# The experts' products of a two-block model in native fp32, on four column strips of TensorE, from raw weights

## What is computed

```python
def swiglu(h, wg, wu, wd):
    return jnp.einsum('...f,fd->...d', jax.nn.silu(h @ wg) * (h @ wu), wd)

def moe_swiglu(h, router, wg, wu, wd):
    ht = h.reshape(B * S, D)                                   # 256 x 1024
    logits = jnp.einsum('td,de->te', ht, router).astype(jnp.float32)
    top_vals, top_idx = lax.top_k(logits, TOP_K)               # TOP_K = 2
    gates = jax.nn.softmax(top_vals, axis=-1)
    ...
    for e in range(N_EXPERTS):                                 # 8
        out = out + dense_gate[:, e:e + 1] * swiglu(ht, wg[e], wu[e], wd[e])
```

## Time and profile before

| | |
|---|---|
| Time, median of 3 runs | 1453.48 us (1453.28 to 1454.73) |
| Span of the profiled execution, first to last instruction | 1449.2 us |
| PE busy / weight loads / DVE / ACT | 1416.9 / 1220.5 / 1104.2 / 905.8 us |
| Granted TensorE clock | 9 or more tenths in each of 40 slices |
| DMA in all | 409.63 MB, mean 283 GB/s |

### The profile page before, as it was taken

One profiled execution on the slowest core, in us unless ns is written; L12 is line 12 of the kernel. 1 busy time (PEld: TensorE's weight loads), 2 busy tenths in 40 slices (PEclk: granted clock), 3 DMA queues, 4 the chain that ended last, 5 costly groups with the idle time before them and its releaser, 6 DMA issues.

```text
span 1449.2 us, 19938 instructions
## 1 busy us (share of the span) xinstructions
PE 1416.9 (98%) x7952; PEld 1220.5 (84%) x7952; DVE 1104.2 (76%) x994; ACT 905.8 (63%) x775; POOL 90.6 (6%) x130
## 2 busy tenths in 40 slices
PE   7999999999998999999999999999999999999998
PEld 6879999897787888888888888888878869788896
DVE  6976454379788889888888888888878894657665
ACT  5664434256647676777777777767766765655653
POOL 3400000034011000000000000000002110000000
PEclk9999999999999999999999999999999999999999
DMA  9569975354569999999999999999999965243341
GB/s 323 165 228 299 330 260 189 118 180 140 210 239 364 382 387 372 357 409 350 379 390 348 401 373 353 406 338 388 387 349 385 390 225 192 88 146 117 117 175 58
DMA packets 120978, 409.63 MB, mean 283 GB/s; under 512 B 7026, under 2 KB 32866, under 8 KB 120912
## 3 DMA queue, kind: packets, MB, share of 16 engines
q1 hardware_dynamic: 114432, 392.32, 73.8%
q0 software_dynamic: 5408, 12.58, 2.7%
q10 hardware_dynamic: 1072, 3.80, 0.7%
HBM read 399.53 MB, written 18.87 MB: 289 GB/s over the span
## 4 chain that ended last, share of the span: by engine, by line
PE 85%; DVE 9%; ACT 3%; DMA 2%; issue 1%; SPq 0%; ACTq 0%; DVEq 0%; POOLq 0%
PE ps L496 22%; PE ps L498 22%; PE ps L497 22%; DVE yT L2047 3%; DVE low L480 2%; PE ps L1190 2%; PE ps L1192 2%; PE ps L1191 2%; PE ps L2749 1%; DMA raw<-in_moe_wu 1%; PE ps L2393 1%; PE ps L1399 1%; PE ps L1397 1%; PE ps L1398 1%; DVE low L486 1%
## 5 line engine op out<-in xcount | busy, mean ns | idle before, releaser
L486 DVE TENSOR_TENSOR low<-raw,high 128x2816 fp32r<-128x2816 f32 (+1 forms) x168 | 516.3, 3089 | 97.1 <-ACT high L475 97.0
L475 ACT ACTIVATE high<-raw 128x2816 fp32r<-128x2816 f32 (+1 forms) x168 | 429.0, 2562 | 108.8 <-PE ps L498 50.5
L496 PE MATMUL ps<-high,xT_hi 128*128 128x512 f32 (+1 forms) x1136 | 419.8, 370 | 8.4 <-DVE low L480 4.2
L498 PE MATMUL ps<-high,xT_lo 128*128 128x512 f32 (+1 forms) x1136 | 415.6, 366 | 0.0
L497 PE MATMUL ps<-low,xT_hi 128*128 128x512 f32 (+1 forms) x1136 | 413.9, 364 | 0.0
L480 DVE TENSOR_TENSOR low<-raw,high 128x2816 fp32r<-128x2816 f32 (+2 forms) x72 | 202.3, 2818 | 74.3 <-ACT high L469 73.1
L496 PEld LDWEIGHTS ps<-high,xT_hi 128*128 128x128 f32 x1136 | 213.3, 188 | 40.6 <-DVE low L480 5.7
L469 ACT ACTIVATE high<-raw 128x2816 fp32r<-128x2816 f32 (+3 forms) x71 | 166.8, 2351 | 117.6 <-PE ps L498 92.0
L497 PEld LDWEIGHTS ps<-low,xT_hi 128*128 128x128 f32 x1136 | 213.6, 188 | 28.0
L498 PEld LDWEIGHTS ps<-high,xT_lo 128*128 128x128 f32 x1136 | 213.1, 188 | 28.3
L496 PE MATMUL ps<-high,eT_hi 128*128 128x512 f32 x352 | 140.7, 400 | 0.0
(11 more groups left out here) (436 smaller groups left out, 1854.0 us busy)
## 6 DMA issues: line engine op xcount, KB each, us to landing
raw<-in_moe_wg SPq DMA_DIRECT2D x64, 1408.0 KB, 8.0
raw<-in_moe_wu SPq DMA_DIRECT2D x64, 1408.0 KB, 9.7
raw<-in_moe_wd SPq DMA_DIRECT2D x48, 1536.0 KB, 8.6
rawb<-in_w_in SPq DMA_DIRECT2D x25, 1024.0 KB, 5.1
raw<-in_w_in SPq DMA_DIRECT2D x16, 1024.0 KB, 9.1
raw<-in_moe_wd SPq DMA_DIRECT2D x16, 1024.0 KB
raw<-in_ffn_wg SPq DMA_DIRECT2D x8, 1408.0 KB, 10.2
raw<-in_ffn_wu SPq DMA_DIRECT2D x8, 1408.0 KB, 9.6
```

The source lines that it names most:

```text
L475: nc.scalar.activation(high[:, j % SPLITS, 0:n], raw[:, j % RAWS, 0:n], ACT.Copy).then_inc(hi_made, 1)
L486: nc.vector.tensor_tensor(low[:, j % SPLITS, 0:n], raw[:, j % RAWS, 0:n], f(high[:, j % SPLITS, 0:n]), ALU.subtract).then_inc(lo_made, 1)
L496: nc.tensor.matmul(out, xh, wh, start=first, stop=False)
L498: return nc.tensor.matmul(out, xl, wh, start=False, stop=last)
```

## The change

The experts' weights are no longer split. Tokens and weights go to TensorE as fp32, an item holds up to 96 tokens, and its stationary operand is a group of 32 tokens. The same 32 tokens are loaded into all four column strips, and each strip moves another quarter of the chunk's columns past them (`by_strips`), so that a PSUM bank holds four column ranges of 32 tokens. The hidden columns are cut 4 x 384 and 4 x 320 (`WIDE`), the down columns 4 x 256. 18 transposes of 128 x 128 turn the hidden values, in two batches (after `j` 8 and `j` 16), and the 8 token transposes follow the second one. The chunks lie in `ering`, eight slots over the former three rings; SP issues chunk `j` when PE has used chunk `j - 8`. Gather products add high and low parts in PSUM. `xs` and `ys` have 13 items of 96 rows.

Beside that: DVE does the whole routing before item 0; the second block's first three chunks are split ahead of `finish` and `add_last_item`; the last item's rows are turned back by 24 fp32 matmuls of 32 rows, and PE waits for `moe_added` 4 ahead of `meta_high`. The eviction's write to `ys` is three DMAs.

```diff
+CAP = 96
+STRIP = 32
+STRIPS, TOKS = P // STRIP, CAP // STRIP
+EXTRA = (2 * T) // (CAP + 1)
...
+WIDE = (384, 320)
+PIECE0 = STRIPS * WIDE[0]
+REST = WIDE[1] - 2 * P
+ESLOTS = 8
+DOWN_N = D // STRIPS
...
+    ering = place("ering", [P, ESLOTS, SLOT], F32, [ring_at])
+    over_spare = [ring_at + ESLOTS * SLOT * 4]
+    y_first = place("y_first", [P, NB, D], F32, over_spare)
+    y_second = place("y_second", [P, NB, D], F32, over_spare)
+    xe = place("xe", [P, KT, CAP], F32, over_spare)
+    drop = place("drop", [P, TOKS, NB, P], F32, over_spare)
...
-    def make_low_item(dve, i, j):
-        dve.wait_ge(hi_made, chunk(i, j + 1))
-        n = words(chunk(0, j))
-        nc.vector.tensor_tensor(low[:, j % SPLITS, 0:n], raw[:, j % RAWS, 0:n], f(high[:, j % SPLITS, 0:n]),
                                 ALU.subtract).then_inc(lo_made, 1)
...
-    def load_item(sp, i, j, src):
-        sp.wait_ge(lo_made, chunk(i, j - RAWS + 1))
-        rows, width = src.shape[1], src.shape[2]
-        sp.dma_start(slot_view(raw, j % RAWS, rows, width), src).then_inc(w_landed[j % RAWS], 16)
...
+            def load_item(i, e, last=False):
+                for j in range(FFN_CHUNKS):
+                    if j == 18 and not last:
+                        load_tokens(i)
+                    sp.wait_ge(w_used, chunk(i, j - ESLOTS + 1))
+                    load_expert(sp, e, j)
...
-            high_upto(MOE0 + 1)
...
+        high2(2)
         finish(n_items, last=True)
-        high2(2)
...
+        pe.wait_ge(moe_added, 4)
...
+            def hidden(i, piece):
+                dve.wait_ge(w_used, chunk(i, 8 * piece + 7) + 1)
+                for t in range(TOKS):
+                    dve.wait_ge(esilu_made, 7 * i + 3 * piece + t + 1)
+                    part = eh[piece][:, t, 0:WIDE[piece]]
+                    nc.vector.tensor_tensor(part, part, ps[:, 3 + t, 0:WIDE[piece]], ALU.mult).then_inc(emult_made, 1)
...
-            low_upto(MOE0 + 5)
-            low_upto(MOE0 + 6)
...
+            def turn_hidden(i, piece):
+                pe.wait_ge(emult_made, MULTS * i + (7 if piece else 3))
+                for jb in range(3):
+                    for t in range(TOKS):
+                        mm = nc.tensor.transpose(ps[:, 3 + jb, t * P:t * P + P], eh[piece][:, t, jb * P:jb * P + P], ident)
+                    mm.then_inc(tp_filled, 1)
...
+            def by_strips(out_of, tokens, weights, n, begins, ends):
+                for s in range(STRIPS):
+                    rows = slice(STRIP * s, STRIP * s + STRIP)
+                    mm = nc.tensor.matmul(out_of(rows), tokens, weights[:, n * s:n * s + n], start=begins, stop=ends, skip_group_check=True)
+                return mm
...
+            def gate_or_up(j):
+                piece, up = j // 8, j // 4 % 2
+                n = WIDE[piece]
+                w = slot_view(ering, j % ESLOTS, 2, STRIPS * n)
+                for k in range(2):
+                    kt = 2 * (j % 4) + k
+                    for t in range(TOKS):
+                        mm = by_strips(lambda rows: ps[rows, 3 * up + t, 0:n], xe[:, kt, STRIP * t:STRIP * t + STRIP], w[:, k, :], n,
+                                       kt == 0, kt == KT - 1)
+                return mm
...
+            def down(j, t, n, tile):
+                w = slot_view(ering, j % ESLOTS, len(DOWN_TILES[j - 16]), D)
+                first = t % 2 * DOWN_N
+                return by_strips(lambda rows: ps[rows, 6 + t // 2, first:first + DOWN_N], eT[:, tile, STRIP * t:STRIP * t + STRIP],
+                                 w[:, n, :], DOWN_N, tile == 0 and t != 1, tile == FT - 1)
...
+                    pe.wait_ge(e_landed[j % ESLOTS], landed(i, j))
+                    gate_or_up(j).then_inc(w_used, 1)
+                    if j == 8:
```

More of the change, by code:

```diff
@@ L431, in model_program, with landed, load_expert, rows @@
     wu_v = a["moe_wu"].rearrange("l e (t p) n -> (l e) p t n", p=P)
-    wd_v = a["moe_wd"].rearrange("l e (t p) n -> (l e) p t n", p=P)
-    def expert_source(e, j):
-        if j < 16:
[L436 to L441, removed]
+    wd_v = a["moe_wd"].rearrange("l e f n -> (l e) f n")
+    LANDINGS = [2 if j in (20, 21, 23) else 1 for j in range(FFN_CHUNKS)]
+    DOWN_TILES = ((0, 1, 2), (3, 4, 5), (6, 7, 8), (9, 10, 11), (12, 13, 14), (15, 16, 17), (18, 19), (20, 21))
+    def landed(i, j):
+        slot = range(j % ESLOTS, FFN_CHUNKS, ESLOTS)
+        before = 16 * MOE0 // RAWS if slot[0] < RAWS else 0
+        return before + 16 * sum(LANDINGS[n] for n in slot if n <= j) + i * (16 * sum(LANDINGS[n] for n in slot))
+    def load_expert(sp, e, j):
+        s = j % ESLOTS
+        def rows(target, source):
+            sp.dma_start(target, source).then_inc(e_landed[s], 16)
+        def tiles(n, first, count):
+            rows(ering[:, s, n * D:(n + count) * D].rearrange("p (t n) -> p t n", t=count),
+                 wd_v[e, first:first + count * P, :].rearrange("(t p) n -> p t n", p=P))
+        def strip(n):
+            return PIECE0 + WIDE[1] * n
+        if j < 16:
+            piece, up, k = j // 8, j // 4 % 2, 2 * (j % 4)
+            width = STRIPS * WIDE[piece]
+            rows(slot_view(ering, s, 2, width), (wg_v, wu_v)[up][e, :, k:k + 2, piece * PIECE0:piece * PIECE0 + width])
+        elif j < 20:
+            tiles(0, 3 * P * (j - 16), 3)
+        elif j == 20:
+            tiles(0, strip(0), 2)
+            tiles(2, strip(1), 1)
+        elif j == 21:
+            tiles(0, strip(1) + P, 1)
+            tiles(1, strip(2), 2)
+        elif j == 22:
+            tiles(0, strip(3), 2)
+        else:
+            ends = wd_v[e, PIECE0:, :].rearrange("(t u q) n -> u q t n", t=2, u=2)
+            for u in range(2):
+                rows(slot_view(ering, s, 2, D)[2 * STRIP * u:2 * STRIP * u + REST, :, :], ends[u, 2 * P:, :, :])
     def chunk(i, j):
@@ new lines, in item @@
+                    gate_or_up(j).then_inc(w_used, 1)
+                    if j == 8:
+                        turn_hidden(i, 0)
+                        if first:
+                            turn_last_places()
+                for j in range(16, FFN_CHUNKS):
+                    if j == 16 and first:
+                        pe.wait_ge(g0_freed, 4)
+                    elif j == 16:
+                        pe.wait_ge(eo_made, 2 * i)
+                    if j == 20:
+                        pe.wait_ge(tp_freed, FREED * i + 7)
+                    pe.wait_ge(e_landed[j % ESLOTS], landed(i, j))
+                    if last and j == FFN_CHUNKS - 1:
+                        for t in range(TOKS):
+                            for n, tile in enumerate(DOWN_TILES[j - 16]):
+                                mm = down(j, t, n, tile)
+                            if t:
+                                mm.then_inc(w_used if t == TOKS - 1 else acc_ready, 1)
+                        return
+                    for n, tile in enumerate(DOWN_TILES[j - 16]):
+                        for t in range(TOKS):
+                            mm = down(j, t, n, tile)
+                    mm.then_inc(w_used, 1)
+                    if j == 16:
+                        turn_hidden(i, 1)
+                        if not last:
+                            turn_tokens(i)
```

531 lines of the change are left out of this document (223 added, 308 removed).

## The result

The changed kernel takes **1470.3 us** in the median (1468.4 to 1472.3, 4 runs) where the kernel before takes 1453.5: ratio **1.0117, 95% interval 1.0102 to 1.0131**. That is slower by 17 us; the forecast was 46 us less (1407, range 1392 to 1440). The profiled execution's span is 1466.5 us against 1449.2.

A forecast was written before the change was run, and what follows sets the result against it. PE (TensorE) was taken to bound the items, with DMA close behind. Strips 38.2, start 4.8 and item 0 4.2, less 0.6 behind the experts, gave 46.6 us: 1407 us from 1453.48, range 1392 to 1440.

The forecast's parts named there:

- The strips: Expert matmuls in four strips: 85.7 us of rounds an item, 4.8 us less an item, 38.2 us in eight.
- The item's 90.2: Forecast time of one expert item on PE, rounds, transposes and switches together, against 94.98 us before.
- the 1.5 us of edges: Edges at transposes and short waits in each item, taken to stay; 0 was their other end.
- strips beside DMA: Rival: strip rounds grow while DMA writes the same memory; at 10% longer, 1476 us; chance 0.07.
- rounds that don't overlap: Rival: each strip round waits for the previous one's drain, 36 us more an item, 1692 us; chance 0.03.
- The 2.84 us in which PE waits for nothing shown as the last item begins are the loop's exit and stay: PE's stop as the last item begins, read as the cost of leaving the item loop, kept unchanged at 2.84 us.
- the DMA rival: Rival: weight transfers bind the items; at 360 GB/s 1436 us; chance 0.12. Against it: 412 GB/s for 36 us.
- The start: Before item 0: DVE's low part removed and a shorter gather (2.8 us) start the experts at 405.4, 4.8 us less.
- Item 0: PE's idle time between 430 and 465 us, behind POOL's scatter and a load, disappears: 4.2 us less.
- The way behind the experts: Last expert matmul to `values`: 13.8 us against 13.2, 0.6 us more, bounds -2 to +3.
- a granted clock below 1.00 would be none of these: Closing remark on signs of a wrong forecast: a lowered clock would belong to none of the named cases.

The follow-up runs named there:

- e5: Changed kernel with TensorE's items 1 to 6 written out and each item's last down chunk loaded in one 128-partition transfer (other rows): 1408.6 us, ratio 0.9697.
- e3: Kernel before, TensorE's loop of six passes over one item made into three passes over two items: 1460.5 us, ratio 1.0044.
- e16: Changed kernel, loop kept, full-width last chunk, a third of weight bytes left out, one of three token groups computed in looped items: 1249.6 us.
- e4: Changed kernel, loop kept, each item's last down chunk loaded by one 128-partition transfer (other rows) in place of two over 64: 1465.5 us, ratio 1.0075.
- e11: Kernel before with TensorE's items 1 to 6 written out instead of looped: 1453.4 us, ratio 1.0013.
- e1: Changed kernel with TensorE's items 1 to 6 written out instead of looped, other engines keeping their loops: 1458.5 us, ratio 1.0044.
- e12: As e5, but the last down chunk, same rows, in two transfers over 64 partitions each: 1461.0 us, ratio 1.0067.
- e8: As e5, with the split of the second block's chunk 2 back behind the last item's eviction: 1406.9 us, ratio 0.9694.
- e13: As e8 with the reference's rows in two 64-partition transfers, the upper half issued by ScalarE once chunk 21 has landed: 1451.5 us, ratio 0.9998.
- e10: As e8 with the reference's rows, the last down chunk in two transfers of one tile over 128 partitions: 1613.1 us, ratio 1.1110.

## Why the prediction was wrong

**The strips** were priced right. Rounds were put at 0.324, 0.2705 and 0.217 and take 0.324, 0.269 and 0.216, also with the DMA at 399 GB/s (e5). The item's 90.2 are 88.49: the 1.5 us of edges went to their other end, nil. The rivals of strips beside DMA and of rounds that don't overlap are out, and with the second the 0.79 of the ideal, an estimate from the Trainium skill (TensorE: Matmul & The Clock Gate, Part 3: Packing small matmuls): in e5 four strips reach 0.99 (0.2133 of 0.216).

**The step that failed first** is "The 2.84 us in which PE waits for nothing shown as the last item begins are the loop's exit and stay". The row was read as the price of leaving a loop, and returning to its head was put at nothing. A stop of this kind is TensorE waiting for code that it doesn't hold: at a return it comes with a long body (e3) and not with a short one (e16). Before, returns were free because 900 matmuls and loads are kept. The change makes that 2,644, and I left this out without counting instructions. With the transfers at full width it costs 57 us (e4 against e5) for five returns, each with its two stops and up to 10 us at half clock. The row itself is not the loop's exit either: 1.98 us stay in e11 and 5.16 in e5, where TensorE has no loop over items 1 to 6.

**The second** is in the DMA rival: 412 GB/s "against it" came from wide transfers, and the new loads were taken to be like them. Chunk 23 is two transfers over 64 partitions, and the rate around it is 238 to 280 GB/s (e1, e12). That alone costs 52 us (e12 against e5); behind the stops it costs 5. The rival had the resource right (chance 0.12) but not its place, and its bound of 1436 was short of e1's 1458.5. The limit of about 358 GB/s for a core in the Trainium skill (DMA: Bandwidth & Descriptors, section Where 436 GB/s comes from) doesn't hold here: e5 moves 399 for 420 us, where the sum needed 392.

**The start** was put at 405.4 and is 406.72: the gather's 32 matmuls of 96 columns take 3.7 us as before, not 2.8. **Item 0** lost its gap, as forecast. **The way behind the experts** was mis-sized: 13.8 forecast, 18.1 measured, because the eviction stands behind ScalarE's `high2(2)` (1187.71 to 1189.62), which waits for a landing, and the 48 records of the last product take 5.5 us at a granted clock of 0.50 where 3 were put. In e8, without that order, 17.7 remain: the wait for the additions and half clock again. It also means that e5's 1408.6 beside a forecast of 1407 is partly luck: the experts gained 46.1 us, the start 4.2, and the way behind them gave back 8.0.

Of "what would show it wrong" the text had "a granted clock below 1.00 would be none of these". That is what came.

Open: why 64 partitions are slow (e13 couldn't tell), and how much of a return's cost is the stop and how much the clock behind it.

## What to carry to other kernels

Before rewriting a loop's work in more, smaller instructions, count a pass on the engine that binds: here 900 and 916 matmuls and loads were kept and 1,800 and 2,644 fetched anew at each return, and writing six items out cost 0.13% (e11). Read a DMA rate from transfers of the same width and shape as the new ones. And when a repair gives little, try it beside the other suspects: here 12 and 5 us were 62 together.

## What the chip showed that I had not expected

- A return to a body that isn't kept stops TensorE for 2.83 and 2.37 us in e3 and for 5.08 and 2.50 at one return of the changed kernel, where the granted clock is 0.50 until 9.5 us behind the first stop. Code that runs straight on is fetched too (50 packets from 600 to 1070 us in e1), with no stop above 1.84 us in items 0 to 6, and with none in them in e5 after 440 us.
- Two transfers over 64 partitions of 512 KB each lower the rate from about 415 to 238 to 280 GB/s for some 20 us (e1, e12), also for the wide ones behind.
- A transfer whose outermost source dimension is 2 ran with a DMA share of 0.13, two of sixteen engines: 53 GB/s (e10).
- Four strips read their weights beside 399 GB/s of DMA without a longer round (e5: 0.216 for 4 x 256 columns; 0.217 in the quiet convolution).
